# Fused attention stage: the turning of the probabilities moved one job later, four probability buffers, and a new split of work between VectorE and ScalarE

## What is computed

```python
s = jnp.einsum('bgrtd,bgcd->bgrtc', qh, kcmp) * scale          # compressed keys: o_cmp and the choice of blocks
_, sel_idx = lax.top_k(imp, k_eff)                             # 8 blocks of 64 keys for each query
...
ss = jnp.einsum('bgrtd,bgtnsd->bgrtns', qb, kb) * scale        # selected blocks
ss = jnp.where(dsel >= 0, ss - sl[..., None, None] * dsel, NEG)
ps = jax.nn.softmax(ss.reshape(B, G, R, T, -1), axis=-1).reshape(ss.shape)
o_sel = jnp.einsum('bgrtns,bgtnsd->bgrtd', ps, vb)
...
sw = jnp.where(wmask, sw - sl[..., None] * dw, NEG)            # window of 512 keys
pw = jax.nn.softmax(sw, axis=-1)
o_win = jnp.einsum('bgrts,bgsd->bgrtd', pw, vwb)
...
o = gt[0] * o_cmp + gt[1] * o_sel + gt[2] * o_win              # gates
```

## Time and profile before

| | us |
|---|---|
| median of 3 runs (lowest, highest) | 3608.7 (3607.91, 3609.65) |
| the profiled execution's own time | 3602.68 |
| its span in the profile | 3600.8 |
| busy in the span: TensorE matmul | 3340.9 (93%) |
| VectorE, ScalarE, GpSimd | 1821.4, 1099.2, 1041.3 |
| first to last instruction of the attention stage | about 861 to 1168 |

### The profile page before, as it was taken

The page is one execution under the profiler, slowest core; times in us unless marked ns, Lnnn a source line. Parts: engine busy times, 40 slices in busy tenths (PEclk is TensorE's granted clock), DMA queues, the critical chain, the costliest instruction groups (busy, mean ns, idle before and its releaser), DMA issues. The chain is left out here.

```text
span 3600.8 us, 56135 instructions
## 1 busy us (share of the span) xinstructions
PE 3340.9 (93%) x22868; PEld 2759.9 (77%) x22868; DVE 1821.4 (51%) x2770; ACT 1099.2 (31%) x1794; POOL 1041.3 (29%) x566
## 2 busy tenths in 40 slices
PE   8999999988888888999999899978887979999999
PEld 7888888866776777888888777758786768888887
DVE  5843656423666547888752335234434264444522
ACT  3112122122555123333333220244332143333321
POOL 2332333335110332222251243222221232222610
PEclk9999999999999999999999899979997989999999
DMA  4353433342000422444363164310011213222621
GB/s 129 131 189 117 131 109 118 112 121 96 9 9 1 161 82 86 150 149 148 121 235 102 47 186 105 117 64 21 20 38 66 86 54 88 82 77 82 239 95 58
DMA packets 323673, 362.77 MB, mean 101 GB/s; under 512 B 25408, under 2 KB 256370, under 8 KB 321962
## 3 DMA queue, kind: packets, MB, share of 16 engines
q1 hardware_dynamic: 293598, 270.33, 24.7%
q10 hardware_dynamic: 28864, 86.66, 6.4%
q0 software_dynamic: 960, 2.21, 0.3%
HBM read 264.11 MB, written 95.03 MB: 100 GB/s over the span
## 5 line engine op out<-in xcount | busy, mean ns | idle before, releaser
L945 PE MATMUL bk<-ffn_bhi,ffn_ahi 128*128 128x512 f32 x1240 | 486.6, 397 | 34.4 <-DVE ffn_alo L1331 10.2
L945 PE MATMUL bk<-ffn_blo,ffn_ahi 128*128 128x512 f32 x1240 | 483.5, 394 | 0.0
L945 PE MATMUL bk<-ffn_bhi,ffn_alo 128*128 128x512 f32 x1240 | 483.2, 394 | 0.0
L211 PE MATMUL acc<-h_hi,whi 128*128 128x512 f32 x1136 | 374.7, 409 | 29.6 <-POOL wlo L171 10.9
L902 POOL TENSOR_TENSOR ffn_alo<-ffn_raw,ffn_ahi 128x512 fp32r<-128x512 f32 x134 | 197.4, 1477 | 670.4 <-ACT ffn_ahi L1098 670.3
L194 POOL TENSOR_TENSOR whi<-raw,ones 128x1024 fp32r<-128x1024 f32 (+1 forms) x83 | 156.5, 1885 | 797.0 <-PE acc L211 567.5
L211 PE MATMUL acc<-h_lo,whi 128*128 128x512 f32 x1136 | 358.5, 395 | 0.0
L211 PE MATMUL acc<-h_hi,wlo 128*128 128x512 f32 x1136 | 357.7, 394 | 0.0
L945 PEld LDWEIGHTS bk<-ffn_bhi,ffn_ahi 128*128 128x128 f32 x1240 | 236.9, 191 | 87.4 <-issue 27.4
L1037 PE MATMUL bk<-ffn_ghi,ffn_dhi 128*128 128x512 f32 x704 | 274.3, 390 | 4.2 <-DVE ffn_glo L1426 2.7
L945 PEld LDWEIGHTS bk<-ffn_bhi,ffn_alo 128*128 128x128 f32 x1240 | 236.5, 191 | 50.5
(11 more groups left out here) (590 smaller groups left out, 6148.6 us busy)
## 6 DMA issues: line engine op xcount, KB each, us to landing
raw<-w_in SPq DMA_DIRECT2D x51, 512.0 KB, 4.1
projT<-proj_stage ACTq DMA_DIRECT2D x51, 512.0 KB, 3.2
ffn_ada_raw<-w_ada SPq DMA_DIRECT2D x12, 2048.0 KB, 9.5
ffn_raw<-w_up SPq DMA_DIRECT2D x44, 512.0 KB, 5.3
ffn_gated<-ffn_gout SPq DMA_DIRECT2D x44, 512.0 KB, 3.3
ffn_graw<-ffn_gated SPq DMA_DIRECT2D x88, 256.0 KB, 3.5
ffn_draw<-w_down SPq DMA_DIRECT2D x31, 512.0 KB, 4.1
ffn_draw<-ffn_w_down SPq DMA_DIRECT2D x31, 512.0 KB, 3.5
```

Source lines behind the costliest of these rows:

```text
L211: last = nc.tensor.matmul(acc[:, t, :], w[:, k, w_cols], x[:, k, t * HALF:(t + 1) * HALF], start=(k == 0 and i == 0), stop=(k == k_tiles - ...
L945: ins = nc.tensor.matmul(o, wt[:, w, k, :], xt[:, x, k, :], start=first and i == 0, stop=last and i == 2, skip_group_check=reopened)
```

## The change

1. There are four probability buffers instead of two (`prob[j % 4]`); `exps(j)` waits for the transposes of job j-4 instead of job j-2.
2. On TensorE the turning stands one job later: `scores(j+2)`, `turns(j-1)`, then `values` on every second j, one job later too.
3. On ScalarE `exps(j+1)` stands ahead of the copy of job j-1, and ScalarE copies only a job's first group.
4. On VectorE `weight(j)` stands ahead of `maxima(j+2)` (before: `weight(j+1)`), the copy of the second group of job j-1 follows, and `output` comes one job later.

```diff
-    prob = [mem.at(f"att_prob{b}", 108 + 8 * b, [P, S]) for b in range(2)]
+    prob = [mem.at(f"att_prob{i}", at, [P, S]) for i, at in enumerate((108, 116, 128, 200))]
@@ tensor engine
-            for j in range(NJ):
+            for j in range(NJ + 1):
                 if j + 2 < NJ:
                     scores(j + 2)
-                turns(j)
-                if j > 1 and j % 2 == 0:
-                    values(j // 2 - 1)
+                if j > 0:
+                    turns(j - 1)
+                if j > 2 and j % 2 == 1:
+                    values((j - 3) // 2)
             values(NJ // 2 - 1)
@@ scalar engine, exps(j)
-                if j >= 2:
-                    n = before[j - 1] - 1
+                if j >= 4:
+                    n = before[j - 3] - 1
                     act.wait_ge(s[f"grouped{n % 2}"], n // 2 + 1)
@@ scalar engine
             exps(0)
-            exps(1)
-            for j in range(NJ):
-                for n in groups_of(j):
-                    copy_group(act, n, lambda o, x: nc.scalar.activation(o, x, ACT.Copy))
-                if j + 2 < NJ:
-                    exps(j + 2)
+            for j in range(NJ + 1):
+                if j + 1 < NJ:
+                    exps(j + 1)
+                if j > 0:
+                    for n in groups_of(j - 1)[0:1]:
+                        copy_group(act, n, lambda o, x: nc.scalar.activation(o, x, ACT.Copy))
@@ vector engine
             maxima(0)
             maxima(1)
-            weight(0)
             for j in range(NJ):
-                if j + 1 < NJ:
-                    weight(j + 1)
+                weight(j)
                 if j + 2 < NJ:
                     maxima(j + 2)
-                if j > 2 and j % 2 == 1:
-                    output((j - 3) // 2)
+                if j > 0:
+                    for n in groups_of(j - 1)[1:2]:
+                        copy_group(dve, n, lambda o, x: nc.vector.tensor_copy(o, x))
+                if j > 3 and j % 2 == 0:
+                    output((j - 4) // 2)
+            for n in groups_of(NJ - 1)[1:2]:
+                copy_group(dve, n, lambda o, x: nc.vector.tensor_copy(o, x))
+            output(NJ // 2 - 2)
             output(NJ // 2 - 1)
```

More of the change, by code:

```diff
@@ L2770, in turns @@
             def turns(j):
-                b = j % 2
-                pe.wait_ge(s[f"scaled{b}"], j // 2 + 1)
+                pe.wait_ge(s[f"scaled{j % 2}"], j // 2 + 1)
                 for n in groups_of(j):
@@ L2776, in turns @@
                     for t in range(nt):
-                        last = nc.tensor.transpose(ps[f"pt{n % 2}"][:, t * P:(t + 1) * P], prob[b][:, (t0 + t) * P:(t0 + t + 1) * P], ident[:])
+                        last = nc.tensor.transpose(ps[f"pt{n % 2}"][:, t * P:(t + 1) * P], prob[j % 4][:, (t0 + t) * P:(t0 + t + 1) * P], ident[:])
                     last.then_inc(s[f"grouped{n % 2}"], 1)
@@ L2825, in exps @@
                 act.wait_ge(s[f"max_done{b}"], j // 2 + 1)
-                if j >= 2:
-                    n = before[j - 1] - 1
+                if j >= 4:
+                    n = before[j - 3] - 1
                     act.wait_ge(s[f"grouped{n % 2}"], n // 2 + 1)
                 n = tiles(i, r) * P
-                nc.scalar.activation(prob[b][:, 0:n], ps[f"sc{b}"][:, 0:n], ACT.Exp, bias=small[b][:, 0:1],
+                nc.scalar.activation(prob[j % 4][:, 0:n], ps[f"sc{b}"][:, 0:n], ACT.Exp, bias=small[b][:, 0:1],
                                      accum_out=small[b][:, 1:2]).then_inc(s[f"exp_done{b}"], 1)
             exps(0)
-            exps(1)
-            for j in range(NJ):
-                for n in groups_of(j):
-                    copy_group(act, n, lambda o, x: nc.scalar.activation(o, x, ACT.Copy))
-                if j + 2 < NJ:
-                    exps(j + 2)
+            for j in range(NJ + 1):
[4 more added lines that the diff above has]
+                        copy_group(act, n, lambda o, x: nc.scalar.activation(o, x, ACT.Copy))
         @block.vector
@@ L2858, in weight @@
                 dve.wait_ge(s[f"inverted{b}"], j // 2 + 1)
-                nc.vector.tensor_scalar(prob[b][:, 0:n], prob[b][:, 0:n], small[b][:, 2:3], N["gates"][:, i, gate:gate + 1],
+                nc.vector.tensor_scalar(prob[j % 4][:, 0:n], prob[j % 4][:, 0:n], small[b][:, 2:3], N["gates"][:, i, gate:gate + 1],
                                         ALU.mult, ALU.mult).then_inc(s[f"scaled{b}"], 1)
```

## The result

The changed kernel takes 3568.0 us (median of 4 runs, 3565.0 to 3569.2) against 3609.2 for the kernel before on the same chip (4 runs): 41 us or 1.2% less, ratio 0.9882 with a 95% interval of 0.9866 to 0.9897. I had predicted 3575.7 in a range of 3555 to 3594. The profiled execution took 3566.9 us, its span 3565.1.

What follows compares the result with a forecast made beforehand. A ring of waits between ScalarE and VectorE, 2.50 us per 5-tile job, bounds the stage; 92 of 128 jobs gain 0.36 us, 33 in all: profiled 3602.7 becomes 3569.7, plus 6.0 for the median, 3575.7 us (3555 to 3594).

Steps and rivals of the forecast that it cites:

- What is late next is an engine's own work: Attention stage after the change: engines' work decides; 5-tile jobs cost VectorE 1.99 us and TensorE 2.09.
- sum of 2.09 us for a 5-tile job: TensorE's scores 0.93 and turning 0.54 twice, values 1.07 and a gap of 0.17: 4.18 us for two jobs.
- uneven hand-over: During values VectorE runs out of scores for some 0.6 us, then catches up; 2.15 us taken for 5 tiles.
- the ring alone: Alternating waits of ScalarE and VectorE in the kernel before: about 0.97 us a job and 0.307 per tile.
- The two exclusions: Jobs gaining nothing: about 26 beside GpSimd's splits of the queries, and 10 where TensorE runs at 1.2 GHz.
- the three that I had named for being wrong: 5-tile jobs above 2.3 us, small jobs beside GpSimd speeding up, or mean clock leaving 0.90 to 0.96.
- the ring of ScalarE and VectorE: Exponentials, next job's weighing and maxima take 2.50 us per 5-tile job; changed, 1.25 us a job, no longer deciding.
- the other chains: Waits kept off by order and buffers; the longest, exponentials, scores, turning, copy, takes 3.1 us for two 5-tile jobs.
- theory A of run 1: Breaking the ScalarE-VectorE ring alone brings nearly the whole gain: 30 to 42 us faster, stage 265 to 277 us.
- the small jobs come free: Clock stays at 2.4 GHz and GpSimd lets weighings by more often: 53 us gained, 3556 us; chance 15%.
- The ring that I had feared: Exponentials queue behind a copy waiting for TensorE; big jobs settle at 2.35 us, 18 us gained, 3591; chance 14%.
- The clock did not stay down: Slower rival: TensorE at 1.2 GHz for over 60% of its work; 70% gives some 20 us, 3629; chance 5%.

Runs made afterwards that it cites:

- run 2: Changed kernel, but ScalarE copies both groups of a job and VectorE none; ratio to the kernel before 0.9862, stage 259.3 us.
- run 9: Changed kernel with two more transposes of 128 columns on TensorE in each of the 64 jobs of 5 tiles or more; ratio to the kernel before 0.9904.
- run 11: Changed kernel with one more unused maximum over 128 columns on VectorE in each of the 64 large jobs; ratio to the kernel before 0.9874.
- run 1: Kernel before with VectorE's order alone changed, weight(j) ahead of maxima(j+2); ratio to the kernel before 1.0004, stage 312.1 us.
- run 5: Changed kernel with VectorE's order undone, weight(j+1) ahead of maxima(j+2) again; ratio to the kernel before 1.0011, stage 312.3 us.
- run 6: Changed kernel with TensorE's order undone, turning job j after scores(j+2) and values one job earlier; ratio to the kernel before 1.0089, stage 340.7 us.
- run 3: Changed kernel with two probability buffers instead of four; ratio to the kernel before 1.0088, stage 334.6 us.
- run 7: Changed kernel with ScalarE's copy of job j-1 ahead of the exponentials of job j+1; ratio to the kernel before 1.0199, median 3678.2 us.
- run 4: Changed kernel with GpSimd's splits of the queries in pieces of 256 columns; ratio to the kernel before 0.9842, stage 246.7 us.
- run 8: Changed kernel with ScalarE copying both groups and GpSimd splitting in pieces of 256 columns; ratio to the kernel before 0.9839, median 3550.8 us.

## Why the prediction came out right, and where its steps were off

**The size.** I forecast 33 us less and 41 were measured (43.5 in the stage).

**The work of the engines** came as summed on VectorE: 224.4 us against 227.5. Its copy of 128 columns takes what the cast of that size did:

```profile
L2881 DVE COPY att_probT<-pt 128x128 f32<-128x128 f32 x39 | 10.9, 281 | 0.3 <-PE pt L2776 0.3
```

The 64 copies last 24.4 us when added one by one, as forecast; busy time rose by 21.3, since instructions on VectorE overlap by a little. ScalarE came to 158.8 us where I had said 150, as its two copies of a job had overlapped too (in the kernel before 0.75 us of busy time for 512 and 128 columns, where the single ones add to 0.86). Neither matters for the time. That the copies cost nothing on the path was right (run 2), and so was that ScalarE's relief brings nothing.

**"What is late next is an engine's own work"** holds: TensorE, by runs 9 and 11. Its sum of 2.09 us for a 5-tile job had left out one gap: there is one of 0.17 us ahead of the values and another ahead of the scores behind them. By the lines of the changed profile that makes 4.30 us for two jobs, 2.15 each. That is the number I took, but with uneven hand-over as the reason. At 6 to 8 tiles I let VectorE lead, 3.1 us at 8, and it does not. With my numbers (2.15, 3.1 and even steps between) the 16 large jobs of a pair of heads would take 38.2 us, and they took 37.0 in the mean of the first three pairs (36.5 by the turnings). The 5-tile jobs of row tile 4 and the mixed ones of row tiles 5 and 6 took 2.15, 2.33 and 2.48 us a job, where my numbers make 2.15, 2.31 and 2.47. At the latter two that is luck, since two transposes more on TensorE, 0.21 us, cost 0.22 and 0.21 us a job there (run 9) and 0.19 us more on VectorE nothing (run 11). What I had too long is the last row tile: 2.1 to 2.4 us a job, not 2.6. The jobs before took a little more than the ring alone, 44.2 against 43.8 us by 0.97 + 0.307 per tile. So the large jobs gained (173.6 - 145.7) / 63 = 0.44 us each where I had 0.35: 28 us instead of 22, and 32 by the turnings. That is the mis-sized term.

**The small jobs** gained 0.38 us each without GpSimd (0.36 said) and, over all 64, 16.4 us (12.4 by the turnings) where 28 of them at 0.36 made 10. The two exclusions were right in kind and too wide. GpSimd's stretches hold 21 or 22 weighings, not 26, and 2 to 4 of those are large jobs of the pair before. For the clock's, 10 us less than before ran at 1.2 GHz, where I had let it stand. The windows there look as in the earlier trace rows:

```profile
945.00:949.00 4.00, 4.00 (x24) 3.34 (x23) 2.25 (x8) 1.48 (x6) 0.00 (x0) 0.50 0.00 0
```

**The signs.** None of the three that I had named for being wrong came: 5-tile jobs are 2.15 us apart, the jobs beside GpSimd are no faster (21 weighings in its 50 us, 22 before), and the mean clock of the stage is 0.94. The stage, 263.7 us, lies below the 270 to 278 that I gave, and the weighings beside GpSimd take 1.52 us in the mean where I had said near 1.

**What each part of the change is for.** I wrote that the ring of ScalarE and VectorE no longer decides, and that the later turning, the buffers and ScalarE's order keep the other chains off. For the whole change that came true. But of those chains I had priced only one, that through ScalarE's copy, and theory A of run 1 took the first ring for the whole bound. Run 1 broke it alone and gained nothing, because the moved weighing closed a ring through TensorE's turning that the kernel before did not have. Runs 5, 6, 3 and 7 each undo one part, VectorE's order, the later turning, the buffers and ScalarE's order, and each loses the whole gain or more. So the change is not one main part with three helpers. Four of its five parts are each needed for any gain with the rest as it is, and only the fifth, VectorE's copies, can be left out.

**The rivals.** That the small jobs come free, 15%, was true in part for the clock, which was low for 10 us less, and not for GpSimd: with its instructions shorter another 17 us come out of the stage (run 4), but not by themselves. The ring that I had feared, exponentials behind a copy that waits for TensorE, is what run 7 makes, and the changed order avoids it. The clock did not stay down; the sum of that rival was a little off, as with 220 us of TensorE work a share of 57% at 1.2 GHz fills the 307 us, and one of 70% makes 338, 31 us more and not 20. The prediction's estimate of 23.0 us for the 64 copies comes to 22.9 when redone. The version of run 4 beats both kernels: 3552.2 us, ratio 0.9842, and run 8 is the same within its interval.

**Open:** how run 4's gain divides between GpSimd and the clock, how much of run 7's loss is the clock's, and whether three buffers would do.

## What to carry to other kernels

When two engines take turns in a wait, count every ring again with the edit in place before pricing the gain: moving one instruction in one engine's order takes it out of one ring and can close another that was not there, and then the two orders have to be moved together. The order in an engine's queue can matter most where the engine is least busy, since a wait at its head holds everything behind it. To find the bound of a stage in which two engines look alike, add the same few microseconds of useless work to each in turn; busy shares left it open here. And divide a stage into parts by the starts on the engine that bounds it: by another engine's starts, work seemed to move between parts where only its lead had changed.

## What the runs showed of the hardware that was not expected

- Cutting GpSimd's instructions from 2.0 to 0.67 us made its work 31% longer (50.8 to 66.3 us) and the stage 17 us shorter. The VectorE weighings beside it fell from 1.52 us in the mean to 0.64, and 44 of them started in the 71 us of splitting, against 21 in 50 us.
- With the small jobs denser the time at 1.2 GHz in the stage fell from 43.2 to 33.2 us, and with GpSimd cut up to 12.3; in run 7, with more waiting on TensorE, it rose to 108.6. The same instructions after the stage took from 2432.5 to 2444.3 us in different profiles: spans of single profiles compare to no better than 10 us here.
- Two independent reciprocals of 128x1 on VectorE start 0.07 us apart, though each shows 0.15 us.
